# The RWKV-7 recurrence on 64x64 blocks, eight heads a group, its inverse applied to the right-hand sides

## The chip, the cores and the metric

One NeuronCore of a Trainium2 chip runs the whole program; the other cores are idle. The metric is the device time of one execution in microseconds (us). TensorE is called PE here, VectorE DVE, ScalarE ACT, GpSimd POOL. A matmul of float32 operands shows in the trace as two records on PE (and two weight loads on PEld), so "records" below are twice the matmul calls of the code.

## The reference, cut to what matters

The program is a long network on 256 tokens of width 1024: two attention layers with feed-forward blocks, then one RWKV-7 layer, a mixture of 32 experts, one more attention layer and a second mixture. The change touches the RWKV-7 recurrence alone, which every one of the 16 heads (64 channels each) runs on its own:

```python
def wkv7_scan(r, w, k, v, a, b):
    # S_t = S_{t-1} diag(w_t) + (S_{t-1} a_t) b_t^T + v_t k_t^T ;  y_t = S_t r_t.
    def step(state, inp):
        r_t, w_t, k_t, v_t, a_t, b_t = inp
        sa = jnp.einsum('bhij,bhj->bhi', state, a_t)
        state = (state * w_t[:, :, None, :] + sa[..., None] * b_t[:, :, None, :]
                 + v_t[..., None] * k_t[:, :, None, :])
        return state, jnp.einsum('bhij,bhj->bhi', state, r_t)
    ...
y = wkv7_scan(rh, jnp.exp(heads(w_log)), kh, vh, -kk, kk * ah)
ym = y.mean(-1, keepdims=True)
yv = jnp.square(y - ym).mean(-1, keepdims=True)
y = ((y - ym) * lax.rsqrt(yv + GN_EPS)).reshape(B, S, D) * gn_g + gn_b
bonus = (jnp.sum(rh * kh * r_k, -1, keepdims=True) * vh).reshape(B, S, D)
return ((y + bonus) * g) @ w_o, v_first
```

## The kernel before

The 256 tokens are two halves of 128; a half holds two chunks of 64 tokens. Within a chunk the recurrence is solved in closed form: score matrices between the tokens of the chunk (products of decayed r, a, k, b), a unit triangular matrix that has to be inverted, and products of the inverse with the values. Between chunks a state Z of 64x64 a head is carried.

The kernel before holds the matrices of both chunks of a half as one 128x128 block-diagonal matrix for each head; the blocks off the diagonal are zero through the masks. Four heads make a group g (their matrices fill one tile `rk_t[g % 2][n]` of 128x512), and two groups, g and g+1, make a "duo", whose steps alternate, so that one group's copies run beside the other group's products. Four duos follow one another: heads 0-7 and 8-15 of the first half of the tokens, then the same of the second half.

PE runs `rk_steps` (L1237), each step for both groups of the duo, on four PSUM banks a group (`rk_bank`):

- `s_ab`, `s_k` (L1125, L1136): scores, operands of 64 rows (the 64 channels of a head), outputs of 128 rows and 128 or 256 columns; even and odd heads lie in rows 0-63 and 64-127.
- `s_ny` (L1143): masked scores times values. The helper `tall` (L1114) takes 128 rows and makes 64 output rows; first all of chunk 0 (c = 0), then all of chunk 1.
- `s_d2` to `s_tt`: the inverse by products of powers, each `four` (L1107): four matmuls of 128x128x128. Order: d2 and its transpose, d4 and transpose, d8, `at` and `b`, t16 and transpose, f and transpose, f2, gt, tt: 56 matmuls a group.
- `s_uw` (L1192): the inverse `tt` times the rows of `ny` and times `rKK`.
- `s_u(c)`, `s_z(c)` for c = 0, 1 and `s_yb`: the walk over the two chunks, 64x64x64 matmuls, each waiting for DVE's update of u or of Z.

DVE masks the scores (`masked`, L2352, two 128x256 operations each), copies some products from PSUM (`v_copy`, L2384), adds the identity (`plus_one`, L2388), and updates u, y and Z (L2420 to L2442). ACT copies the other products (`rk_copy`, L1622). Every hand-over is a semaphore that counts the steps in the lists `RK_PE`, `RK_DVE`, `RK_ACT` (L102 to L106): PE's step waits (`need`) for DVE's or ACT's copy of the step it reads.

Ahead of each half PE transposes the operands (`rk_transposes`, L1083), and ACT (L1648) and DVE (L2450) copy them to AR and BK; the second half's transposes wait for the `yb` updates of the first. Behind the last duo comes the group norm: POOL (`group_norms`, L2583) does the quarters 0 to 2 as they come free, DVE the last one (L2464 to L2474, 128x512 operations), then PE transposes y (`transposes("y_r")`), multiplies it by `wo_r`, and the layer norm and the experts follow.

Weights stream through a ring of six units of 1 MB, loaded by the SP queue as PE sets units free; the recurrence itself sets none free.

Of the kernel before, what the change touches and what calls it, by code (L numbers as in the profile page):

```python
# [12 lines left out]
ALU = mybir.AluOpType  # L13
# [3 lines left out]
P = 128  # L17
# [33 lines left out]
def shape_constants():  # L51
# [4 lines left out]
    def halves(m):  # L56
# [8 lines left out]
    sub = row // SUB == col // SUB  # L65
# [6 lines left out]
        "sub_lower": sub & (row > col),  # L72
        "sub_upper": sub & (row < col),
        "off_lower": chunk & ~sub & (row > col),
        "chunk_upper": chunk & (row < col),
        "chunk_upto": chunk & (row <= col),
# [25 lines left out]
RK_PE = ["ab", "abt", "k", "ny", "d2", "d2t", "d4", "d4t", "d8", "at", "b", "t16t", "t16", "f", "ft", "f2", "gt", "tt",  # L102
         "u0", "w1", "u_0", "z_0", "u_1", "z_1", "yb"]
RK_DVE = ["de", "dtm", "mk", "d2", "dti", "d4t", "d2i", "d8i", "d4ti", "at", "t16t", "f", "f2i", "fti", "tt", "w1",
          "u_0", "z_0", "u_1", "z_1", "yb"]
RK_ACT = ["ny", "d2t", "d4", "b", "t16", "ft", "gt", "u0"]  # L106
# [90 lines left out]
def build(nc, A, out):  # L197
    ctx = ExitStack()
    with ctx:
# [74 lines left out]
        rk_n = [_tiles[18][:, 0:256], _tiles[18][:, 256:512]]  # L274
# [158 lines left out]
        gn_root = sem("gn_root")  # L433
        gn_done = sem("gn_done")
# [60 lines left out]
        def rk_heads(g):  # L495

            return [(2 * par + pp, par, pp, 2 * (g % 4) + pp, 2 * (2 * (g % 4) + pp) + par)
                    for par in range(2) for pp in range(2)]
# [31 lines left out]

        def rk_cols(buf, g, par):

            v = buf[:].rearrange("p t (r q d) -> p t r q d", q=2, d=HD)
            return v[:, g // 4, 2 * (g % 4):2 * (g % 4) + 2, par, :]
# [115 lines left out]
        def _(pe):  # L650
# [432 lines left out]
            def rk_transposes(t):  # L1083

                pe.wait_ge(rk_in, t + 1)
                if t:
                    for g in (2, 3):
                        rk_wait(pe, "dve", g, "yb")
                        rk_wait(pe, "act", g, "u0")
# [24 lines left out]
            def tall(o, c, c0, lhs, i, rhs, signal):  # L1114

                mm(o[HD * c:HD * c + HD, c0:c0 + HD], lhs[:, i * P + HD * c:i * P + HD * c + HD], rhs, signal=signal)
# [6 lines left out]

            def s_ab(g):
                if g >= 2 and g != 4 and g != 5:  # L1125
                    need(g - 2, "yb", "u0")
                for i, par, pp, r, h in rk_heads(g):
                    q = slice(HD * par, HD * par + HD)
                    mm(rk_bank(g, par)[:, pp * P:(pp + 1) * P], AR[q, r, 0, :], BK[q, r, 0, :],
                       signal=rk_pe[g % 2] if i == 3 else None)  # L1130
                for i, par, pp, r, h in rk_heads(g):
                    q = slice(HD * par, HD * par + HD)
                    mm(rk_bank(g, 2 + par)[:, pp * SEQ:(pp + 1) * SEQ], BK[q, r, 0, :],
                       AR[q, r, :, :].rearrange("p x t -> p (x t)"), signal=rk_pe[g % 2] if i == 3 else None)

            def s_k(g):  # L1136
                need(g, dve="de")
                for i, par, pp, r, h in rk_heads(g):
                    q = slice(HD * par, HD * par + HD)
                    mm(rk_bank(g, par)[:, pp * SEQ:(pp + 1) * SEQ], BK[q, r, 1, :],  # L1140
                       AR[q, r, :, :].rearrange("p x t -> p (x t)"), signal=rk_pe[g % 2] if i == 3 else None)

            def s_ny(g):  # L1143
                need(g, dve="mk")
                for c in range(2):
                    for x, tile in enumerate((5, 6)):
                        for i, par, pp, r, h in rk_heads(g):
                            tall(rk_bank(g, 2), c, x * SEQ + i * HD, rk_t[g % 2][tile], i,
                                 rV[:, g // 4, h * HD:(h + 1) * HD], rk_pe[g % 2] if c and x and i == 3 else None)

            def s_d2(g):
                four(g, 0, 1, 0, True)
                four(g, 1, 0, 1, True)

            def s_d4(g):
                need(g, "d2", "d2t")
                four(g, 0, 4, 3, True)
                four(g, 1, 3, 4, True)

            def s_d8(g):  # L1160
                need(g, "d4t", "d4")
                four(g, 3, 6, 5, True)

            def s_at(g):
                need(g, "d2i", "ny")
                four(g, 0, 3, 1, True)
                need(g, "d4ti")
                four(g, 1, 6, 7, True)

            def s_t16(g):  # L1170
                need(g, "at", "b")
                four(g, 2, 4, 0, True)
                four(g, 3, 0, 4, True)

            def s_f(g):
                need(g, "t16t", "t16")
                four(g, 0, 5, 2, True)
                four(g, 1, 2, 5, True)

            def s_f2(g):  # L1180
                need(g, "f", "ft")
                four(g, 2, 3, 1, True)

            def s_gt(g):
                need(g, "fti")
                four(g, 0, 0, 3, True)

            def s_tt(g):
                need(g, act="gt")
                four(g, 1, 7, 4, True)  # L1190

            def s_uw(g):  # L1192
                need(g, "tt", "ny")
                tt = rk_t[g % 2][2]
                for c in range(2):
                    for i in range(4):
                        tall(rk_bank(g, 2), c, i * HD, tt, i, rk_n[g % 2][:, i * HD:(i + 1) * HD],
                             rk_pe[g % 2] if c and i == 3 else None)
                for i, par, pp, r, h in rk_heads(g):
                    mm(rk_bank(g, 3)[HD * par:HD * par + HD, pp * P:(pp + 1) * P],  # L1200
                       rKK[:, g // 4, h * HD:(h + 1) * HD], tt[:, i * P:(i + 1) * P],
                       signal=rk_pe[g % 2] if i == 3 else None)

            def s_u(c):
                def step(g):
                    need(g, "z_0" if c else "w1", "u0")
                    if g >= 4 and c == 0:
                        need(g - 4, "z_1")
                    t = slice(CH * c, CH * c + CH)
                    for par in range(2):  # L1210
                        for x in range(2):
                            for pp in range(2):
                                r, q = 2 * (g % 4) + pp, slice(HD * par, HD * par + HD)
                                lhs = AR[q, r, 1, t] if x else rk_t[g % 2][6][q, SEQ + pp * P + CH * c:SEQ + pp * P + CH * c + CH]
                                mm(rk_bank(g, par)[t, x * P + pp * HD:x * P + (pp + 1) * HD], lhs, Z[q, r, :],
                                   signal=rk_pe[g % 2] if par and x and pp else None)
                return step

            def s_z(c):
                def step(g):  # L1220
                    need(g, f"u_{c}")
                    t = slice(CH * c, CH * c + CH)
                    for i, par, pp, r, h in rk_heads(g):
                        o = rk_bank(g, 2)[HD * par:HD * par + HD, pp * HD:(pp + 1) * HD]
                        hc = slice(h * HD, (h + 1) * HD)
                        mm(o, rA[t, g // 4, hc], rk_t[g % 2][5][t, i * HD:(i + 1) * HD], True, False)
                        mm(o, rK[t, g // 4, hc], rV[t, g // 4, hc], False, True,
                           signal=rk_pe[g % 2] if i == 3 else None)
                return step

            def s_yb(g):
                for c in range(2):
                    for i in range(4):
                        tall(rk_bank(g, 3), c, i * HD, rk_t[g % 2][8], i, rk_t[g % 2][5][:, i * HD:(i + 1) * HD],
                             rk_pe[g % 2] if c and i == 3 else None)

            rk_steps = [s_ab, s_k, s_ny, s_d2, s_d4, s_d8, s_at, s_t16, s_f, s_f2, s_gt, s_tt, s_uw,  # L1237
# [65 lines left out]
            for g in (6, 7):  # L1303
                rk_wait(pe, "dve", g, "yb")
# [1440 lines left out]
```

## Time and profile before

| | us |
|---|---|
| three runs | 2927.4, 2938.86, 2939.47 |
| median of the three | 2938.86 |
| the profiled execution, its own time | 2947.6 |
| its span in the trace | 2945.7 |
| first score matmul of the recurrence | at 1374.06 |
| last update of y (L2442) ends | at 1589.24 |
| PE busy, share of the span | 85% |

The profiled execution is 8.7 us above the median. In the lists of rows "out<-in" are tiles by the program's names with the buffer numbers left out (B3 is B), `128*64 128x64` on PE is rows times columns of the weights and then partitions times elements of the moving operand; busy is the union of the records' times, the mean is that of one record's length, and a record's length contains some 0.2 us of pipeline, so the rate is read from starts, not from lengths. The time behind "idle before" in brackets names what the engine waited for.

### The profile page before, as it was taken

How to read it: one execution, taken by the hardware profiler on the slowest of the kernel's cores; microseconds unless marked ns; L12 is line 12 of the kernel's file. 1: busy time of each engine (PE TensorE's matmuls, PEld its weight loads, DVE VectorE, ACT ScalarE, POOL GpSimd, SP SyncE). 2: the span in 40 equal slices, each digit the busy share in tenths (PEclk: the TensorE clock that was granted, in tenths of full speed). 3: DMA queues.
4: the chain of work that ended last, by engine and by line, in shares of the span. 5: the costliest groups of instructions: out<-in, count | busy, mean ns of one | idle time of the engine just before them, and what ended most of it. 6: DMA issues, size and time to landing. Idle time of an engine off the chain costs nothing. (4 is left out here: it accounts for less than half of the span.)

```text
span 2945.7 us, 38153 instructions
## 1 busy us (share of the span) xinstructions
PE 2516.4 (85%) x14696; PEld 1765.7 (60%) x14696; DVE 1508.1 (51%) x2095; ACT 721.9 (25%) x1031; POOL 892.5 (30%) x540
## 2 busy tenths in 40 slices
PE   7998769987997799798888689889868868888985
PEld 7986659967996699545886333333347654343432
DVE  7875669768955597427564412222156463212123
ACT  4324433333334333112111110101023321011110
POOL 6888878888800285000233000000001000000000
PEclk9999889988998899897999799999988789999998
DMA  8666347655652365332001499999954127999995
GB/s 296 230 230 218 109 152 256 249 188 210 235 196 77 117 241 215 136 119 90 1 2 44 153 420 420 422 422 421 421 198 143 58 74 321 419 418 422 421 422 249
DMA packets 109853, 694.82 MB, mean 236 GB/s; under 512 B 14424, under 2 KB 15768, under 8 KB 34856
## 3 DMA queue, kind: packets, MB, share of 16 engines
q1 hardware_dynamic: 88704, 618.23, 53.5%
q0 software_dynamic: 21024, 74.99, 7.3%
q8 instruction: 79, 1.29, 0.2%
q14 instruction: 32, 0.25, 0.0%
q10 hardware_dynamic: 14, 0.06, 0.0%
HBM read 692.12 MB, written 1.11 MB: 235 GB/s over the span
## 5 line engine op out<-in xcount | busy, mean ns | idle before, releaser
L666 PE MATMUL bank<-ring,B 128*64 128x512 f32 (+1 forms) x3264 | 781.1, 598 | 113.1 <-DMA ring<-in_moe_wgate 67.8
L1839 DVE TENSOR_TENSOR ring_r<-ring,B_r 128x2048 fp32r<-128x2048 f32 x184 | 539.5, 2951 | 213.2 <-ACT B_r L1400 213.0
L666 PEld LDWEIGHTS bank<-ring,B 128*64 128x64 f32 (+1 forms) x3264 | 269.0, 140 | 582.5 <-issue 569.6
L666 PE MATMUL bank<-B_r 128*128 128x512 f32 (+1 forms) x1928 | 512.0, 352 | 17.5 <-DVE B L2082 9.7
L1400 ACT ACTIVATE B_r<-ring 128x2048 fp32r<-128x2048 f32 x184 | 347.0, 1909 | 322.6 <-PE bank L666 320.1
L666 PE MATMUL bank<-xt_r,B_r 128*128 128x256 f32 x1408 | 401.1, 285 | 23.8 <-issue 8.9
L666 PEld LDWEIGHTS bank<-B_r 128*128 128x128 f32 x1928 | 333.4, 193 | 110.8 <-issue 56.9
L666 PE MATMUL bank<-xt_r,ring_r 128*128 128x256 f32 x1408 | 399.0, 283 | 0.0
L666 PEld LDWEIGHTS bank<-xt_r,B_r 128*128 128x128 f32 x1408 | 269.0, 191 | 26.8 <-issue 24.7
L666 PEld LDWEIGHTS bank<-xt_r,ring_r 128*128 128x128 f32 x1408 | 270.5, 192 | 0.0
L664 PE MATMUL bank<-const,B 128*128 128x128 f32 x688 | 127.9, 351 | 138.2 <-issue 25.0
L666 PE MATMUL bank<-B 128*128 128x128 f32 (+7 forms) x1536 | 188.6, 315 | 40.8 <-DVE B L2355 11.3
L2567 POOL TENSOR_TENSOR wkx<-wkx,small_s 128x1024 f32<-128x1024 f32 x84 | 201.2, 2405 | 66.9 <-DMA wkx<-in_ada_w 55.5
L666 PE MATMUL bank<-B_r,xt_r 128*128 128x512 f32 x416 | 174.9, 421 | 43.0 <-DVE lo_r L1850 23.0
L664 PEld LDWEIGHTS bank<-const,B 128*128 128x128 f32 x688 | 111.2, 188 | 155.6 <-issue 89.9
L666 PEld LDWEIGHTS bank<-B 128*128 128x128 f32 (+4 forms) x1536 | 162.3, 198 | 63.2 <-issue 15.3
L2093 DVE TENSOR_TENSOR B<-bank,B 128x512 f32<-128x512 f32 x128 | 79.7, 683 | 234.5 <-PE bank L666 234.4
L666 PE MATMUL bank<-lo_r,B_r 128*128 128x256 f32 x704 | 199.2, 283 | 0.0
L2120 DVE TENSOR_TENSOR B_r<-bank,B_r 128x512 fp32r<-128x512 f32 x64 | 41.2, 686 | 273.0 <-ACT B_r L1511 273.0
L666 PE MATMUL bank<-ring_r,xt_r 128*128 128x512 f32 x416 | 171.9, 413 | 0.0
L2660 POOL DMA_DIRECT2D rows<-mod_rows x14 | 7.7, 553 | 496.9 <-DVE small_s L1752 462.2
L2111 DVE SCALAR_TENSOR_TENSOR B<-B,bank 128x512 f32<-128x512 f32 x32 | 36.5, 1140 | 226.0 <-issue 185.2
(328 smaller groups left out, 3263.0 us busy)
## 6 DMA issues: line engine op xcount, KB each, us to landing
ring<-in_moe_wgate SPq DMA_DIRECT2D x128, 1024.0 KB, 8.5
ring<-in_moe_wup SPq DMA_DIRECT2D x128, 1024.0 KB, 8.7
ring<-in_moe_wdown SPq DMA_DIRECT2D x128, 1024.0 KB, 9.9
ring<-in_ffn_w_gate SPq DMA_DIRECT2D x44, 1024.0 KB, 4.8
ring<-in_ffn_w_up SPq DMA_DIRECT2D x44, 1024.0 KB, 5.0
ring<-in_ffn_w_down SPq DMA_DIRECT2D x44, 1024.0 KB, 4.9
wkx<-in_ada_w POOLq DMA_DIRECT2D x72, 512.0 KB, 6.0
B<-in_ada_w POOLq DMA_DIRECT2D x24, 512.0 KB, 8.2
```

Of the source, the lines that this page charges most:

```text
L664: ins = pe.transpose(out, lhsT, rhs)
L666: ins = pe.matmul(out, lhsT, rhs, start=start, stop=stop, skip_group_check=True)
L1400: act.activation(hi, ring[:, slot, :], ACT.Copy).then_inc(sp_hi, 1)
L1839: dve.tensor_tensor(ring_r[:, slot, :], ring[:, slot, :], f32(hi), ALU.subtract).then_inc(sp_lo, 1)
L2093: dve.tensor_tensor(y, bank[4 + 2 * t + e][:, :], y, ALU.add).then_inc(mo_acc, 1)
L2111: dve.scalar_tensor_tensor(out=strided(m_h, 4), in0=natural(m_sg, 4), scalar=m_slot[(n // 2) % 2][:, j:j + 1], in1=natural(bank[1][:, :], ...
L2120: dve.tensor_tensor(ye_lo[:, c], bank[2 + d][:, :], f32(ye_hi[:, c]), ALU.subtract)\
L2567: pool.tensor_tensor(w, w, cs[:, 2 * t:2 * t + 2].unsqueeze(2).to_broadcast([P, 2, BANK]), ALU.mult).then_inc(mod_chain, 1)
L2660: pool.dma_start(bc[n % NROW], row_source(name).partition_broadcast(P)).then_inc(row_landed[n % NROW], 16)
```

## The change

- The constant masks shrink from 128x128 to 128x64 (two 64x64 blocks, one for each chunk), and a matrix of 128x128 with two zero blocks becomes a tile of 128x64: rows 0-63 are chunk 0, rows 64-127 chunk 1. A tile of 128x512 so holds eight heads, and a group is eight heads: four groups in all, in two rounds ("half") in place of four duos.
- `four` and `tall` go. `chunks` makes every product: for each of eight heads, a 64x64x64 matmul in rows 0-63 to output rows 0-63, then one in rows 64-127 to output rows 64-127 of the same bank. The scores too are made in 64x64 (or 64x64x128) pieces, alternating over both halves of rows and columns.
- The inverse is not formed. Its last factors are applied to the right-hand sides: `s_f` computes f, its transpose and two products with the right-hand sides (`y`), `s_z1` squares f (transposed) and applies the next factor, `s_uw` the last one. The steps t16, gt, f2 and tt leave; at, d8 and b become single products.
- `s_d2` moves ahead of `s_ny`.
- DVE's and ACT's copies are as wide as before (512 columns) and serve eight heads; some are additions now (`v_plus`, `v_z1`).
- Group norm: POOL does quarters 0 and 1 (the first half), DVE the whole second half in 128x1024 operations, with POOL's gate and bonus for it kept in `lo`.

The diff, cut to its core:

```diff
-            def four(g, x, lhs, rhs, sig):
-                for i in range(4):
-                    c = slice(i * P, (i + 1) * P)
-                    mm(rk_bank(g, x)[:, c], rk_t[g % 2][lhs][:, c], rk_t[g % 2][rhs][:, c],
-                       signal=rk_pe[g % 2] if i == 3 else None)
+            def chunks(o, lhs, rhs, signal, c0=0):
+                for i in range(8):
+                    for c in range(2):
+                        t, x = slice(CH * c, CH * c + CH), slice(i * CH, (i + 1) * CH)
+                        mm(o[t, x], lhs[t, x], rhs[t, c0 + i * CH:c0 + (i + 1) * CH],
+                           signal=signal if i == 7 and c else None)
+            def product(g, x, lhs, rhs):
+                tiles = rk_t[g % 2]
+                chunks(rk_bank(g, x), tiles[lhs], tiles[rhs], rk_pe[g % 2])
+            def scores(g, x, side):
+                v = rk_bank(g, x)[:, :].rearrange("p (r x s) -> p r x s", x=2, s=CH)
+                o = rk_bank(g, x + 1)[:, :].rearrange("p (r x s) -> p r x s", x=2, s=CH)
+                for i, r in rk_pairs(g):
+                    for c in range(2):
+                        t = slice(CH * c, CH * c + CH)
+                        for par in range(2):
+                            q = slice(HD * par, HD * par + HD)
+                            mm((v, o)[par][t, i, :, :], BK[q, r, side, t], both(AR[q, r, :, :], c),
+                               signal=rk_pe[g % 2] if i == 3 and c and par else None)
 ...
+            def s_d2(g):
+                need(g, dve="dtm")
+                product(g, 2, 1, 0)
+                product(g, 3, 0, 1)
 ...
+            def s_at(g):
+                need(g, "dti", "ny")
+                product(g, 0, 3, 1)
             def s_d8(g):
                 need(g, "d4t", "d4")
-                four(g, 3, 6, 5, True)
+                product(g, 1, 6, 5)
+            def s_b(g):
+                need(g, "d8i")
+                product(g, 2, 6, 7)
+            def s_t16t(g):
+                need(g, "b")
+                product(g, 3, 4, 0)
             def s_f(g):
-                need(g, "t16t", "t16")
-                four(g, 0, 5, 2, True)
-                four(g, 1, 2, 5, True)
-            def s_f2(g):
-                need(g, "f", "ft")
-                four(g, 2, 3, 1, True)
-            def s_gt(g):
-                need(g, "fti")
-                four(g, 0, 0, 3, True)
-            def s_tt(g):
-                need(g, act="gt")
-                four(g, 1, 7, 4, True)
+                need(g, act="t16t")
+                product(g, 0, 5, 2)
+                product(g, 1, 2, 5)
+                h, cols = rk_cols(g)
+                chunks(rk_bank(g, 2), rk_t[g % 2][5], rk_n[g % 2], None)
+                chunks(rk_bank(g, 3), rk_t[g % 2][5], rKK[:, h, cols], rk_pe[g % 2])
+            def s_z1(g):
+                need(g, dve="ft")
+                product(g, 0, 1, 3)
+                need(g, act="y")
+                chunks(rk_bank(g, 2), rk_t[g % 2][3], rk_t[g % 2][6], None)
+                chunks(rk_bank(g, 3), rk_t[g % 2][3], rk_t[g % 2][7], rk_pe[g % 2])
             def s_uw(g):
 ...
+                need(g, "z1")
+                product(g, 0, 2, 0)
+                w, tt = rk_t[g % 2][4], rk_t[g % 2][2]
+                for x in range(4):
+                    for c in range(2):
+                        for par in range(2):
+                            i, t = 2 * x + par, slice(CH * c, CH * c + CH)
+                            k = slice(i * CH, (i + 1) * CH)
+                            mm(rk_bank(g, 1 + c)[HD * par:HD * par + HD, x * CH:(x + 1) * CH], w[t, k], tt[t, k],
+                               signal=rk_pe[g % 2] if x == 3 and c and par else None)
 ...
-            rk_steps = [s_ab, s_k, s_ny, s_d2, s_d4, s_d8, s_at, s_t16, s_f, s_f2, s_gt, s_tt, s_uw,
+            rk_steps = [s_ab, s_k, s_d2, s_ny, s_d4, s_at, s_d8, s_b, s_t16t, s_f, s_z1, s_uw,
                         s_u(0), s_z(0), s_u(1), s_z(1), s_yb]
 ...
-            for duo in range(4):
-                if duo % 2 == 0:
-                    rk_transposes(duo // 2)
+            for half in range(TB):
+                rk_transposes(half)
                 for step in rk_steps:
-                    for g in (2 * duo, 2 * duo + 1):
+                    for g in (2 * half, 2 * half + 1):
                         step(g)
 ...
-            h, c, n = quarter(3)
-            y, hs = rR[:, h, c], slice(n, n + 8)
+            y, sq16, hs = heads(rR, 1), B[9][:, 0, :].rearrange("p (h d) -> p h d", d=HD), slice(H, 2 * H)
```

In `s_u` and `s_z` the two halves of rows (or of output rows) alternate matmul by matmul, where before one half's matmuls came first.

## Rows read from the trace of the kernel before

**Rows 1.** The page of the profile: busy time; DMA share in each of 40 slices.

```profile
PE 2516.4 (85%) x14696; PEld 1765.7 (60%) x14696; DVE 1508.1 (51%) x2095; ACT 721.9 (25%) x1031; POOL 892.5 (30%) x540
...
DMA  8666347655652365332001499999954127999995
```

**Rows 2.** Busy time of each engine in stretches; "x" counts instruction records, PEclk is granted clock.

```profile
core 0: us, PE busy (x) PEld busy (x) DVE busy (x) ACT busy (x) POOL busy (x), PEclk, DMA share, GB/s
1374.00:1589.20 215.20, 188.84 (x2208) 179.98 (x2208) 132.08 (x316) 40.84 (x85) 55.01 (x75) 0.97 0.02 5
1374.00:1386.40 12.40, 9.51 (x112) 8.84 (x112) 8.09 (x24) 0.72 (x3) 2.49 (x2) 0.86 0.06 24
1434.00:1441.00 7.00, 7.00 (x76) 6.88 (x75) 1.15 (x4) 1.44 (x6) 6.42 (x8) 0.60 0.01 2
...
1479.00:1485.06 6.06, 3.85 (x36) 3.53 (x34) 3.09 (x7) 2.06 (x4) 4.50 (x9) 1.00 0.01 4
```

**Rows 3.** PE in order of time (start, length, shapes, records, idle before): 128x128x128 products.

```profile
1402.20 1.06 PE L666 MATMUL bank<-xt,wkx 128*128 128x128 f32 x8
1403.10 1.06 PE L666 MATMUL bank<-wkx,xt 128*128 128x128 f32 x8
```

**Rows 4.** The same view: 64-column products, first in one half, then across two.

```profile
1492.64 1.72 PE L666 MATMUL bank<-B 128*64 128x64 f32 x29 [2.83 <-DVE B L2355]
1494.15 0.27 PE L666 MATMUL bank<-B,wkx 128*64 128x64 f32 x1
...
1494.25 0.22 PE L666 MATMUL bank<-B,wkx 128*64 128x64 f32 x1
1494.26 0.22 PE L666 MATMUL bank<-B 128*64 128x64 f32 x1
1494.31 0.22 PE L666 MATMUL bank<-B,wkx 128*64 128x64 f32 x1
1494.32 0.22 PE L666 MATMUL bank<-B 128*64 128x64 f32 x1
```

**Rows 5.** The same view: expert products in two column halves, then full width.

```profile
1761.46 2.79 PE L666 MATMUL bank<-ring,B 128*64 128x512 f32 x12 [0.91 <-DMA ring<-in_moe_wgate]
...
1603.82 2.74 PE L666 MATMUL bank<-ring,xt 128*128 128x512 f32 x6
```

**Rows 6.** Groups of instructions by shape, 1374 to 1600 us: DVE, ACT and one of PE.

```profile
L2384 DVE COPY B<-bank 128x512 f32<-128x512 f32 x24 | 16.5, 688 | 37.7 <-PE bank L666 37.7
...
L666 PE MATMUL bank<-B 64*128 64x256 f32 x128 | 16.2, 384 | 0.0
L1624 ACT ACTIVATE B<-bank 128x512 f32<-128x512 f32 x24 | 14.3, 597 | 53.6 <-PE bank L666 53.6
...
L2355 DVE TENSOR_TENSOR B<-bank,const 128x256 f32<-128x256 f32 x40 | 14.2, 413 | 2.3 <-PE bank L666 2.3
```

**Rows 7.** PE in order of time: the starts at which it had stood idle, and for whom.

```profile
1381.64 0.58 PE L666 MATMUL bank<-B 128*64 128x64 f32 x3 [2.83 <-DVE B L2355]
...
1411.01 0.71 PE L666 MATMUL bank<-B 128*128 128x128 f32 x4 [1.38 <-DVE B L2388]
...
1419.12 0.96 PE L666 MATMUL bank<-B 64*64 64x64 f32 x16 [0.38 <-DVE B L2422]
...
1485.06 0.39 PE L666 MATMUL bank<-B 64*128 64x128 f32 x2 [1.43 <-DVE B L2450]
```

**Rows 8.** DVE in order of time, at the end of the recurrence; last, a 1024-wide group before it.

```profile
1589.33 0.69 DVE L2464 TENSOR_REDUCE small_s<-B 128x8 f32<-128x512 f32 x1
...
1594.35 0.69 DVE L2474 TENSOR_TENSOR B<-B,mix_t 128x512 f32<-128x512 f32 x1
...
L2338 DVE TENSOR_TENSOR B<-B 128x1024 f32<-128x1024 f32 x2 | 2.4, 1216 | 0.0
```

**Rows 9.** The chain that ended last, in order of time, behind the recurrence.

```profile
1595.30 3.65 PE bank L664 x16
...
1599.78 29.54 PE bank L666 x64
```

More of the change, by code:

```diff
@@ L64, in shape_constants @@
     chunk = row // CH == col // CH
-    sub = row // SUB == col // SUB
+    at, to = row % CH, np.arange(CH)[None, :]
+    sub = at // SUB == to // SUB
     aug = p % 64
@@ L1122, in need, with both @@
                     rk_wait(pe, "act", g, act)
-            def s_ab(g):
[L1125 to L1134, printed above, removed]
+            def both(v, c):
+                return v[:, :, CH * c:CH * c + CH]
@@ L1136, in s_k @@
+            def s_ab(g):
+                for i, r in rk_pairs(g):
+                    for c in range(2):
+                        t = slice(CH * c, CH * c + CH)
+                        for par in range(2):
+                            q = slice(HD * par, HD * par + HD)
+                            mm(rk_bank(g, par)[t, i * CH:(i + 1) * CH], AR[q, r, 0, t], BK[q, r, 0, t],
+                               signal=rk_pe[g % 2] if i == 3 and c and par else None)
+                scores(g, 2, 0)
             def s_k(g):
@@ L1137, in s_k @@
                 need(g, dve="de")
[L1138 to L1141, printed above, removed]
+                scores(g, 0, 1)
+            def s_d2(g):
+                need(g, dve="dtm")
+                product(g, 2, 1, 0)
+                product(g, 3, 0, 1)
@@ L1143, in s_ny @@
             def s_ny(g):
                 need(g, dve="mk")
[L1145 to L1153, printed above, removed]
@@ L1204, in s_u @@
             def s_u(c):
                 def step(g):
-                    need(g, "z_0" if c else "w1", "u0")
-                    if g >= 4 and c == 0:
-                        need(g - 4, "z_1")
+                    need(g, "z_0" if c else "z1", "w1")
                     t = slice(CH * c, CH * c + CH)
[L1210 to L1216, printed above, removed]
+                    w = rk_t[g % 2][6][:, :].rearrange("p (r s) -> p r s", r=4)
@@ new lines, in step @@
+                    for side in range(2):
+                        for x, r in rk_pairs(g):
+                            for par in range(2):
+                                q = slice(HD * par, HD * par + HD)
+                                lhs = AR[q, r, 1, t] if side else w[q, x, t]
+                                mm(rk_bank(g, par)[t, side * SEQ + x * HD:side * SEQ + (x + 1) * HD], lhs, Z[q, r, :],
+                                   signal=rk_pe[g % 2] if par and side and x == 3 else None)
@@ L1644, in _ @@
-            for duo in range(4):
-                if duo % 2 == 0:
-                    for b in range(4):
-                        act.wait_ge(wt_pe, 8 * (duo // 2) + b + 1)
-                        act.activation(AR[:, 2 * b:2 * b + 2, :, :].rearrange("p r x t -> p (r x t)"), bank[b][:, :],
-                                       ACT.Copy).then_inc(wt_act, 1)
-                for step in (rk_ny, rk_step("d2t", 4, 1), rk_step("d4", 5, 0), rk_step("b", 4, 1),
-                             rk_step("t16", 7, 3), rk_step("ft", 3, 1), rk_step("gt", 4, 0), rk_u0):
-                    for g in (2 * duo, 2 * duo + 1):
+                h, cols = rk_cols(g)
@@ new lines, in rk_ny, with rk_y, rk_w1 @@
+                rk_copy(g, "ny", rk_n[g % 2], 0)
+                rk_copy(g, "ny", rR[:, h, cols], 1).then_inc(rk_act[g % 2], 1)
+            def rk_y(g):
+                rk_copy(g, "y", rk_t[g % 2][6], 2)
+                rk_copy(g, "y", rk_t[g % 2][7], 3).then_inc(rk_act[g % 2], 1)
+            def rk_w1(g):
+                rk_wait(act, "pe", g, "w1")
+                w = rk_t[g % 2][6][:, :].rearrange("p (r s) -> p r s", r=4)
+                for c in range(2):
+                    v = bank[4 * (g % 2) + 1 + c][:, 0:SEQ].rearrange("p (r s) -> p r s", r=4)
+                    ins = act.activation(w[:, :, CH * c:CH * c + CH], v, ACT.Copy)
+                ins.then_inc(rk_act[g % 2], 1)
@@ new lines, in _ @@
+            for half in range(TB):
+                for b in range(4):
+                    act.wait_ge(wt_pe, 8 * half + b + 1)
+                    act.activation(AR[:, 2 * b:2 * b + 2, :, :].rearrange("p r x t -> p (r x t)"), bank[b][:, :],
+                                   ACT.Copy).then_inc(wt_act, 1)
+                for step in (rk_step("d2", 3, 2), rk_ny, rk_step("d4", 5, 2), rk_step("t16t", 5, 3), rk_y,
+                             rk_step("u0", 5, 0), rk_w1):
+                    for g in (2 * half, 2 * half + 1):
@@ new lines, in v_yb @@
+                h, cols = rk_cols(g)
+                sig(dve.tensor_tensor(rR[:, h, cols], rkb(g, 2)[:, :], rR[:, h, cols], ALU.add), g)
+            for half in range(TB):
+                dve.wait_ge(rk_in, TB)
+                for b in range(4):
+                    dve.wait_ge(wt_pe, 8 * half + 4 + b + 1)
+                    dve.tensor_copy(BK[:, 2 * b:2 * b + 2, :, :].rearrange("p r x t -> p (r x t)"),
+                                    bank[4 + b][:, :]).then_inc(wt_dve, 1)
+                for step in (v_de, v_dtm, v_mk, v_copy("d2t", 4, 3), v_dti, v_copy("d4t", 6, 3),
+                             v_plus("at", 0, 0, "dti", 1), v_one("d8", 7, 1), v_plus("b", 4, 2, "d8i", 7), v_f,
+                             v_copy("ft", 3, 1), v_one("f2t", 2, 0), v_z1, v_u(0), v_z(0), v_u(1), v_z(1), v_yb):
+                    for g in (2 * half, 2 * half + 1):
```

242 lines of the change are left out of this document (109 added, 133 removed).

## The prediction, made before the changed kernel ran

> **What bounds the kernel now.** I read the page first: PE is busy 85% of the span and DMA is the wall only in the expert stages, while around slice 19 to 21 the DMA share is 0 [rows 1]. So in the recurrence nothing but PE and its partners can be late. The stretches say more [rows 2]: from PE's first score matmul to the last update of y pass 215.2 us, in which PE is busy 188.8, DVE 132, ACT 41, and DMA moves 5 GB/s because the ring is full. PE's order of time shows why it is not more [rows 7]: in each duo it waits 2.8 us for the masks (L2355), 1.4 us for an added identity (L2388), 0.4 for u (L2422), the copies after the transposes 1.4 us, and one stretch between the halves takes 6.1 us [rows 2]. The 2.8 us waits also cost clock: behind one, 7 us ran at 0.60 of the full clock [rows 2]. Behind the recurrence the chain runs on through DVE's norm, the transposes and `wo_r` without a gap [rows 8, 9]; the experts' loads wait for units that `wo_r` frees, so a microsecond saved in the recurrence arrives at the end in full. I take that at one to one: the ring is full in both kernels.
>
> **The price of a record.** Everything hangs on this. A 128x128x128 product takes 0.90 us for 8 records, 112 ns each [rows 3]: two passes of the 128 columns. A record with 64 columns takes 0.06 us, 58 before rounding (1494.25 to 1494.31 of one stream) [rows 4]. So half the columns cost half, but half the rows or half the output rows buy nothing by themselves: a 64x64x64 product has 1/8 of the work of a 128x128x128 one and half its price. Eight heads in two chunks need 16 of them (32 records), where eight heads needed 8 full ones (16 records): 32 x 58 = 1.86 us against 16 x 112 = 1.79 us. Without overlap the blocks win nothing.
>
> They do overlap. Where the `tall` products pass from output rows 0-63 to 64-127, two streams run side by side: starts at .25, .26, .31, .32, that is two records in 58 ns [rows 4]. The expert products, which alternate over the two column halves, show it without end: 12 records of 512 columns in 2.79 us, against 6 in 2.74 us at full width [rows 5]. Halves of the rows overlap too: 128 score records of 256 columns and 64 rows were busy 16.2 us, 127 ns each, where two passes of 256 columns alone would take 225 [rows 6]. No row shows a pair that differs in both and writes one bank, as `chunks` makes it, nor more than a few 64-column pairs in line. Bounds for a record: 29 ns (two perfect streams) and 58 ns (one stream). I take 31, by the pair in rows 4, with a little for each first record; 29 to 36 belongs to the forecast.
>
> **Part by part.** *PE.* Before, a group of four heads has 136 matmuls, 56 of them full; eight groups, 2176 records (the trace has 2208 with some neighbours [rows 2]). After, a group of eight heads has ab 32, k 16, d2 32, ny 32, d4 32, at, d8, b and t16t 16 each, f 64, z1 48, uw 32, u and z 64, yb 16: 432 matmuls, 864 records; four groups, 3456 records. At 31 ns that is 107 us of PE, in place of 188.8.
>
> *DVE and ACT.* The copies are as wide as before (690 ns on DVE, 600 on ACT, 413 for 256 columns [rows 6]) and serve twice the heads. A group costs DVE 12 masks at 0.34 us apart, 11 wide operations at 0.60 apart, u and z 2 x 2.0, yb 0.7: about 16 us, 63 for the four. It is no bound in sum. ACT has 10 operations a group, about 6 us.
>
> *The waits.* I walked the new order step by step with these durations, two groups in turn; a step of 32 records is 1.0 us, and the way through a copy and back is 0.26 (pipeline) + 0.69 + 0.05, also 1.0 us, so single-product steps (at, d8, b, t16t) just hide it. The mask wait of 2.8 us goes: `s_d2` needs only dtm and now lies ahead of `ny`, and ab, k and d2 cover DVE's masks but for 0.3 us. `s_z1` is covered by the long `s_f`. The added first wait is z1's for ACT's y: f of the other group (4 us) is queued ahead of it, cost nothing; if it were not hidden it would be 1.2 us twice a half. What is late next is u and z: DVE's four 64x256 operations take 1.4 us against PE's 1.0, so each pass over u and z stands some 0.8 us, together 3.2 us a half. So a half is 1728 x 31 = 53.6, + 3.2 = 56.8 us, + 0.9 for DVE's last yb.
>
> *Between and around.* The 6.1 us between the halves stay [rows 2]; two of the four duo starts vanish with their mask waits. At the start PE is on the low clock (0.86 over the first 12.4 us [rows 2]); I allow 1.5 us. Sum: 56.8 + 6.1 + 57.7 + 1.5 = 122.1 us against 215.2: 93.1 saved.
>
> *Group norm.* DVE's last norm now has 1024 columns: seven operations of 0.70 become 1.22 [rows 8], + 3.6 us, all on the path. POOL's part is shorter and ends in the first half's shadow; its three gate steps at the start (some 15 us) lie beside PE's work and may slow a mask a little, 0 to 1 us. Net 89.5 us. Smaller constants, and the additions in place of copies: nothing.
>
> The profiled execution took 2947.6 us, its like after would be 2858; the runs' median is 8.7 lower, so against it 2938.9 - 89.5 = **2849.4**, I say 2850. At 29 ns a record the walk gives 2844 (stalls grow as PE shrinks), at 36 it gives 2864.
>
> **The rivals.** (a) *The supply of instructions or the turn-around is slower than two full streams*, say 45 ns a record. For it: pairs in line were never seen longer than four, and the rate of records doubles against the 2208 in 215 us. Halves of 78.5 us, net 46 saved: 2893.
> (b) *Two row halves on one bank take turns.* In every place of the old kernel where row halves alternate, they write different banks; `chunks` alone (1216 of a half's 1728 records) writes one. Those at 58 ns, the rest at 31: 86.4 + 1 us a half, 183 in all, net 29 saved: 2910. The Trainium skill, "TensorEngine Tiling (Array Packing)", Restrictions and Gotchas, says this: different row tiles cannot access the same PSUM bank at the same time. By that rule 2910 holds; the trace has no case for or against it, since its overlaps on one bank share their rows.
> (c) *No overlap at all*, 58 ns: halves of 100 us, 209 in all, net 3 saved: 2936. Against it rows 4, 5 and 6.
> The Trainium skill, "TensorE: Matmul & The Clock Gate", section on 56 against 53.3 ns, names a decoding mode in which every matmul costs 62 ns; by that page the sum would be an estimated 214 us for PE and 2949 in all; the two records in 58 ns of rows 4 speak against it.
> (d) *The blocks use less of the array and the clock stays low*, at 1.2 GHz: a pair in 107 ns, 54 each, 196 us, net 16: 2923. Against it: 215 us of mixed shapes had a mean clock of 0.97, and the low stretches follow idle time [rows 2].
> (e) *Every change of half costs a restart: slower.* The first record of a new stream is 0.05 us longer than those behind it (0.27 at 1494.15, 0.22 then [rows 4]). If that were lost time and no overlap came of it, each matmul in `chunks` and its kin would pay it, as the half changes with each; the mean record is then 58 + 25 = 83 ns: 286 us of PE, 82 us more: 3021. It decides from a mean of 58.5 ns on. Against it: the alternating expert products lose nothing [rows 5].
>
> **How the numbers follow.** Forecast 0.66 (2844 to 2864), (a) 0.14, (b) 0.08, (c) 0.04, (d) 0.03, (e) 0.05. The range reaches from 2838 (29 ns, less the 6 us by which a run may lie low) to 2898 (case a and as much above) and leaves out b to e, 0.20. Half a per cent, 15 us, is about what a measurement of this kernel can tell from no change. Faster by more: forecast, a, b and half of d, 0.90. Same: c and the rest of d, 0.05. Slower: e, 0.05.
>
> **What would show it.** In the profile of the changed kernel: PE's records in the recurrence about 3456 at a mean spacing near 31 ns, pairs of starts a few ns apart all through `chunks`; idle spots of PE before u and z, none of 2.8 us; granted clock near 1 past the first microseconds; a norm tail of some 9.5 us in place of 5.9. `chunks` at 58 ns with scores near 30 would be (b); spacing in bursts with no waits between would be (a); a DVE that is never idle would mean that I sized the copies wrong.

## The result, and the profile after

| | before | changed |
|---|---|---|
| median of the runs, us | 2935.48 (4 runs, 2927.4 to 2939.47) | 2851.39 (4 runs, 2836.06 to 2853.56) |
| ratio, with its 95% interval | | 0.9701 (0.9664 to 0.9738) |
| second comparison, on one chip | 2933.11 (11 runs) | 2836.47 (5 runs), ratio 0.9667 (0.9641 to 0.9692) |
| first score matmul to last update of y, us | 215.2 | 113.6 (second profile 114.4) |
| PE idle between y's last matmul and its transposes, us (start to start) | 6.8 | 10.9 |

The changed kernel is 84 us faster by the first comparison, 97 by the second; 2850 was forecast. The page of the changed kernel, where [rows 1] stood before:

```profile
PE 2421.3 (85%) x15976; PEld 1682.0 (59%) x15976; DVE 1432.9 (51%) x1927; ACT 704.3 (25%) x991; POOL 879.8 (31%) x520
...
DMA  7765436765764156533102799999933129999995
```

The windows of the recurrence, to be read beside [rows 2] (the same columns): the whole, its first 5.4 us, the long middle part of the first half, and the stretch between the halves.

```profile
core 0: us, PE busy (x) PEld busy (x) DVE busy (x) ACT busy (x) POOL busy (x), PEclk, DMA share, GB/s
1374.60:1488.20 113.60, 104.84 (x3488) 101.96 (x3488) 70.20 (x148) 23.58 (x45) 43.52 (x55) 1.00 0.03 10
1374.60:1380.00 5.40, 5.18 (x209) 4.92 (x211) 4.65 (x14) 0.00 (x0) 5.09 (x5) 1.00 0.10 39
1380.00:1414.50 34.50, 34.38 (x1206) 34.24 (x1202) 19.02 (x33) 8.62 (x16) 7.80 (x6) 1.00 0.02 4
1427.40:1433.70 6.30, 3.89 (x40) 3.57 (x36) 3.17 (x5) 2.06 (x4) 5.44 (x11) 1.00 0.00 0
```

1280 more records than before, and PE is busy 84 us less: 104.8 against 188.8. What PE was not busy in fell too, from 26.4 to 8.8 us. The clock was at 1.00 from the first score matmul on. The middle part shows the price: 34.5 us with 1206 records, 28.6 ns each, with hardly a pause. In order of time, two steps made by `chunks` (two products each), the step `s_uw`, and the score matmuls with 128 columns (group by shape):

```profile
1383.26 2.03 PE L672 MATMUL bank<-B 64*64 64x64 f32 x64
1385.13 2.03 PE L672 MATMUL bank<-B,wkx 64*64 64x64 f32 x64
...
1411.70 1.61 PE L672 MATMUL bank<-B 64*64 64x64 f32 x64
1413.15 1.03 PE L672 MATMUL bank<-xt 64*64 64x64 f32 x29
```

```profile
L672 PE MATMUL bank<-B 64*64 64x128 f32 x256 | 8.1, 270 | 0.6 <-issue 0.6
```

From 1383.26 to 1385.13 pass 1.87 us for 64 records: 29.2 ns each, the price of `chunks`. In `s_uw` (from 1411.70 to 1413.15) the first 32 records are a product of `chunks`, some 0.93 us at that price; the other 32, w1, use all four quarters of the array in turn and have the remaining 0.52 us, about 16 ns each. They draw the mean of the middle part down. 256 score records were busy 8.1 us, 32 ns each, though each has twice the columns; the scores use all four quarters too.

PE's order of time, the longer waits, first half and the stretch behind it (beside [rows 7]):

```profile
1379.48 2.08 PE L672 MATMUL bank<-B 64*64 64x64 f32 x64 [0.22 <-DVE xt L2375]
...
1415.59 1.15 PE L672 MATMUL bank<-Z,B 64*64 64x64 f32 x32 [0.87 <-ACT B L1661]
...
1418.24 1.15 PE L672 MATMUL bank<-B 64*64 64x64 f32 x32 [0.57 <-DVE B L2451]
...
1423.20 1.15 PE L672 MATMUL bank<-B 64*64 64x64 f32 x32 [0.36 <-DVE B L2451]
...
1428.57 3.68 PE L670 MATMUL bank<-const,B 128*128 128x128 f32 x32 [0.99 <-DVE B L2469]
```

The 2.8 us for the masks are 0.22; what is late is now ACT's copy of w1 (0.87), then DVE's u (0.57 and 0.36). The wait for yb ahead of the transposes is 1.0 us, where it was 0.8. In the second profile the same waits stand in the same places; only ACT's is shorter in the first half, 0.56. DVE's norm at the end, beside [rows 8]; in between lie the like rows at 1489.52, 1490.78 and 1492.04 and 0.8 us of small operations:

```profile
1488.27 1.22 DVE L2486 TENSOR_REDUCE small_s<-B 128x16 f32<-128x1024 f32 x1
...
1494.03 1.23 DVE L2494 TENSOR_TENSOR B<-B,small_s 128x1024 f32<-128x1024 f32 x1
1495.29 1.23 DVE L2496 TENSOR_TENSOR B<-B 128x1024 f32<-128x1024 f32 x1
1496.55 1.23 DVE L2497 TENSOR_TENSOR B<-B,lo 128x1024 f32<-128x1024 f32 x1
```

### The profile page after: what moved, and what is told of

Same layout as the page of the kernel before. It is cut to its first block, busy times and chain, and to the rows that moved or that the text cites. A ratio compares the mean times of both kernels' runs of the same rounds, so it can differ in the third digit from the quotient of the medians.

```text
span 2834.2 us, 40407 instructions
## 1 busy us (share of the span) xinstructions
PE 2421.3 (85%) x15976; PEld 1682.0 (59%) x15976; DVE 1432.9 (51%) x1927; ACT 704.3 (25%) x991; POOL 879.8 (31%) x520
## 4 chain that ended last, share of the span: by engine, by line
PE 48%; DMA 26%; DVE 9%; POOL 8%; issue 6%; ACT 2%; SPq 1%; POOLq 0%; DVEq 0%; ACTq 0%
PE bank L672 46%; DMA ring<-in_moe_wup 11%; DMA ring<-in_moe_wgate 11%; POOL wkx L2592 2%; DMA wkx<-in_ada_w 2%; PE bank L670 2%; POOL wkx L2596 2%; POOL wkx L2598 1%; DVE ring_r L1857 1%; POOL B L2592 1%; SPq L582 1%; POOL mix_t L2601 1%; POOL B L2604 0%; DMA B<-in_ada_w 0%; DMA const<-in_const 0%
## 5 line engine op out<-in xcount | busy, mean ns | idle before, releaser
L1857 DVE TENSOR_TENSOR ring_r<-ring,B_r 128x2048 fp32r<-128x2048 f32 x184 | 526.7, 2882 | 221.1 <-ACT B_r L1416 220.8
L672 PE MATMUL bank<-B 64*64 64x64 f32 (+6 forms) x2272 | 126.8, 253 | 20.2 <-ACT B L1480 5.4
L672 PE MATMUL bank<-ring_r,B_r 128*128 128x512 f32 x352 | 138.9, 395 | 0.0
```

Source lines behind the costliest of these rows:

```text
L672: ins = pe.matmul(out, lhsT, rhs, start=start, stop=stop, skip_group_check=True)
L1857: dve.tensor_tensor(ring_r[:, slot, :], ring[:, slot, :], f32(hi), ALU.subtract).then_inc(sp_lo, 1)
```

## The experiments

### The price of a stream by itself

The kernel `bench` leaves out everything of the reference: it holds only streams of 64 float32 matmuls (128 records), each behind a short wait. Its loop (`row half`, `output half`, bank, columns, for matmul i):

```python
s["one"]       = [(0, 0, 1, 64)] * n
s["diagonal"]  = [(i % 2, i % 2, 2, 64) for i in range(n)]
s["same_rows"] = [(0, i % 2, 3, 64) for i in range(n)]
s["same_out"]  = [(i % 2, 0, 4 + i % 2, 64) for i in range(n)]
s["four"]      = [(i % 2, (i // 2) % 2, 6 + i % 2, 64) for i in range(n)]
s["runs2"]     = [((i // 2) % 2, (i // 2) % 2, 2, 64) for i in range(n)]   # runs4, runs8 alike
s["four_32"]   = [(i % 2, (i // 2) % 2, 6 + i % 2, 32) for i in range(n)]
```

> Only streams of float32 matmuls of 64x64x64, 64 of them (128 records) each, nothing of the reference is computed. Spacing of records in ns that the theory expects (two streams in different row or output halves run side by side; a stream alone takes 58; the engine looks about four records ahead): one tile 58; the two diagonal tiles in turn on one bank 29; same rows, output halves in turn, one bank 29; rows in turn, same output half, two banks 29; all four tiles in turn 15; diagonal in runs of 2 matmuls 29; runs of 4, 29 to 36; runs of 8, about 45; four tiles with 32 columns 15, if the weight load of 64 columns is as long as the matmul, 8 if not. Rival (one bank is shared badly by two row halves): the first diagonal stream at 58. Rival (the supply of instructions ends somewhere near 29): all four tiles no faster than 25.

PE in order of time, one row a stream in the order one, diagonal, same_rows, same_out, four, runs2, runs4, runs8, four_32:

```profile
22.58 7.67 PE L62 MATMUL bank<-X 64*64 64x64 f32 x128 [0.40 <-DVE t L71]
30.57 3.95 PE L62 MATMUL bank<-X 64*64 64x64 f32 x128 [0.32 <-DVE t L71]
34.85 3.95 PE L62 MATMUL bank<-X 64*64 64x64 f32 x128 [0.33 <-DVE t L71]
39.13 3.95 PE L62 MATMUL bank<-X 64*64 64x64 f32 x128 [0.33 <-DVE t L71]
43.41 2.21 PE L62 MATMUL bank<-X 64*64 64x64 f32 x128 [0.33 <-DVE t L71]
45.96 4.16 PE L62 MATMUL bank<-X 64*64 64x64 f32 x128 [0.35 <-DVE t L71]
50.44 4.99 PE L62 MATMUL bank<-X 64*64 64x64 f32 x128 [0.32 <-DVE t L71]
55.74 6.42 PE L62 MATMUL bank<-X 64*64 64x64 f32 x128 [0.32 <-DVE t L71]
62.48 2.07 PE L62 MATMUL bank<-X 64*64 64x32 f32 x128 [0.32 <-DVE t L71]
```

This is one execution; its granted clock was 1.00 in the window of each of these streams. A row's length, less the 0.22 us of its last record, over 127 steps: 58.7 ns for one tile; 29.4 for the diagonal on one bank, for two output halves and for two row halves; 15.7 for all four tiles; runs of 2, 4 and 8 matmuls 31.0, 37.6 and 48.8; four tiles with half the columns 14.6. So a tile (a quarter of the array, 64 rows by 64 output rows) takes 58.7 ns a record alone and the same beside one other; with all four at work it takes 62.8 (4 x 15.7), so the tiles are all but independent. The diagonal on one bank is as fast as any pair, so the rival of the shared bank falls. The last stream shows that instructions can come at one record in 14.6 ns. With 32 columns a record is nearly as long as with 64: what is left is the weight load of 64 columns, or the rate of supply, which this run does not tell apart. A run of 8 matmuls (16 records) takes 16 x 48.8 = 781 ns where alone it would take 939: the next tile begins some 160 ns, nearly three records, ahead of the end. The expected spacings were met within 4 ns; the runs of 2, 4 and 8 came out the dearest against them (29, 29 to 36 and about 45 were expected).

### The same work, one half of the array after the other

```diff
-                for i in range(8):
-                    for c in range(2):
+                for c in range(2):
+                    for i in range(8):
                         t, x = slice(CH * c, CH * c + CH), slice(i * CH, (i + 1) * CH)
```

> The changed kernel with the two loops in chunks swapped: all eight heads of chunk 0 first, then all eight of chunk 1. The same matmuls, copies and waits; only the order within a product differs. Theory (the gain is the overlap of the two halves of the array, and a new stream starts when about four records of the old one are left): a chunks record costs (32 - 4) x 58 / 32 = 51 ns instead of 29; 2432 such records, + 53 us of PE, of which 3 to 5 us fill stalls that exist already: about + 48, 2900 us. Rival (the gain comes from fewer waits, fewer rounds and the cheaper algebra, the order within a product is indifferent): within 5 us of the changed kernel, 2851. Second rival (no overlap unless matmuls alternate one by one): 58 ns, + 66, 2917.

Measured: 2892.37 us, ratio 0.982 (0.9762 to 0.9878), in its own comparison with the kernel before (2935.07). Against the changed kernel's ratios, 0.9701 and 0.9667, that is 35 and 45 us more. Windows of its recurrence, the whole and the long middle part of the first half:

```profile
1371.79:1529.50 157.71, 149.46 (x3488) 146.91 (x3488) 69.06 (x148) 24.11 (x45) 42.75 (x55) 0.99 0.02 8
1376.68:1432.08 55.40, 55.40 (x1215) 55.40 (x1216) 19.29 (x34) 8.73 (x16) 7.53 (x7) 1.00 0.01 3
```

The recurrence took 157.7 us, 44.1 more than the changed kernel's 113.6, from two swapped loops. In the middle part 1215 records take 55.4 us, 45.6 ns each, w1 among them. Steps made by `chunks` alone, 64 records each, follow one another every 3.02 us (at 1382.94, 1385.95 and 1388.97): 47.1 ns a record. 51 was expected; 48.8 is what `bench` gives for runs of eight matmuls. The 17.9 ns above 29.2, for 2432 such records, make 43.5 us, nearly the whole difference. The look-ahead is seen as well: from 1382.71 to 1382.88 the last three records of one tile start in turn with the first three of the next. Idle time is 8.3 us, where it was 8.8. The rival that the order is indifferent falls; so does the one that needs strict alternation (58 ns).

The second kernel orders the scores, u, z and w1 so too (each loop over the halves `c` and `par` pulled outside the loop over the heads, as above):

> As the last one, and the scores, u, z and w1 are also ordered so that each quarter or half of the array gets all its matmuls before the next one does. Theory: on top of the 51 ns of chunks, the scores go from 21 to about 56 ns a record (runs of 8 records, 4 of them overlapped), u and w1 to 36, z to 51: together 171 us of PE against 100, less 5 us of stalls filled: + 66, about 2917. If it comes out at 2936 or above, the 64x64 form without overlap wins nothing or loses, as the prediction's case c says. If it stays below 2880, the recurrence got shorter for another reason than overlap.

Measured: 2899.32 us, ratio 0.9868 (0.9815 to 0.992).

```profile
1372.50:1545.40 172.90, 167.98 (x3488) 166.77 (x3488) 69.54 (x148) 24.00 (x45) 42.67 (x55) 1.00 0.02 6
```

PE busy 168.0 us, where 171 was worked out; the recurrence took 172.9, + 59.3. The 2917 expected in all was too much by 18 us: the recurrence grew by 59 and not 66, and the 2917 was built on the changed kernel's first median, which lay 15 us above its second. Against the kernel before the recurrence is still 42.3 us shorter: 20.9 of PE and 21.4 of idle time; less the 4.1 us of the longer norm that makes 38, and the medians differ by 36 (2935.07 to 2899.32). That PE's share is a gain at all is put down to what the look-ahead hides at each change of tile (48.8 against 58.7 ns, or 1.56 us a product of eight heads against the 1.79 of [rows 3]); the other share is the waits. A 64x64 form with no overlap whatever could not be made, since the engine looks ahead by itself; by an estimate from `bench` it would cost 3456 x 58.7 = 203 us of PE, more than the old form's 188.8. This also speaks against the new algebra as the cause: counted in products of eight heads, the inverse and its application were 16 before and are 17 now (w1 and u0 taken in), so applying the factors instead of forming the inverse saves PE none of them. What it does for the waits was not tried by itself.

### The overlap alone, in the kernel before

The kernel before with its 64-row and 64-column matmuls in turn; `rk_heads` lists the heads with `par` inside, and `tall` is called with `c` inside:

```diff
-                for c in range(2):
-                    for i in range(4):
+                for i in range(4):
+                    for c in range(2):
                         tall(rk_bank(g, 3), c, i * HD, rk_t[g % 2][8], i, rk_t[g % 2][5][:, i * HD:(i + 1) * HD],
```

(the same in `s_ny` and `s_uw`; in `s_u` and `s_z` the loop over `par` goes innermost)

> The kernel before, block-diagonal 128x128 matrices and all, with one thing of the change alone: its 64-row or 64-column matmuls (scores, ny, uw, u, z, yb) alternate between the two halves, one by one. Theory: ny, uw and yb fall from some 50 to 30 ns a record, u and z are soon held by DVE's updates: 3 to 4 us a duo, together - 12 us (- 8 to - 18), 2923 us. Rival (the new order alone is worth a large part of the 84 us): below 2900. Rival (DVE's waits take it all back): within 3 us of 2935.

Measured: 2930.73 us, ratio 0.9976 (0.9948 to 1.0005), 12 runs.

```profile
1366.60:1572.90 206.30, 175.26 (x2208) 163.92 (x2208) 133.15 (x317) 40.86 (x85) 56.10 (x75) 0.97 0.02 5
```

The recurrence took 206.3 us, 8.9 less. PE is busy 13.6 us less, and 4.7 of that comes back as idle time. Of that 2.2 us stand before the added identity (12.0 in all against 9.8, the longest 2.3 against 1.4), since DVE's work ahead of it takes as long as before, and only 0.3 before u (2.7 against 2.4). The rival of a large part (below 2900) falls. The other (within 3 us of 2935) can't be refuted by the timing, whose interval reaches from 15 us less to 1 more; it is the trace that shows the 8.9 us. The order pays only where matmuls leave a part of the array free: 112 of the 272 records of a group were full 128x128 ones with nothing to run beside.

### The step that was moved

```diff
-RK_PE = ["ab", "abt", "k", "d2", "d2t", "ny", "d4",
+RK_PE = ["ab", "abt", "k", "ny", "d2", "d2t", "d4",
-            rk_steps = [s_ab, s_k, s_d2, s_ny, s_d4,
+            rk_steps = [s_ab, s_k, s_ny, s_d2, s_d4,
```

(and ACT copies ny ahead of d2)

> The changed kernel with s_ny ahead of s_d2, as in the kernel before. Theory (the move hides DVE's masks): PE ends k at 4.4 us, the masks for ny are ready 7.7 us after the first score matmul, so PE stands 3.3 us in each half where it stood 0.5; + 2.8 twice, and if the idle time brings the low clock back as in the kernel before, some 2.5 us more in each half: + 6 to + 10, 2857 to 2861. Rival (the masks are hidden anyway, for the copies behind would wait the same): + 0 to + 1.

Measured: 2859.74 us, ratio 0.9726 (0.9673 to 0.9779). Two waits of PE, and windows of the whole recurrence and of the 6 us behind the first wait:

```profile
1379.94 3.53 PE L672 MATMUL bank<-B 64*64 64x64 f32 x64 [2.87 <-DVE B L2375]
...
1443.12 2.48 PE L672 MATMUL bank<-B 64*64 64x64 f32 x64 [2.28 <-DVE B L2375]
```

```profile
1372.40:1493.50 121.10, 107.74 (x3488) 104.68 (x3488) 68.77 (x148) 23.58 (x45) 42.59 (x55) 0.97 0.03 9
1379.90:1386.00 6.10, 6.06 (x158) 6.06 (x160) 1.31 (x4) 1.70 (x4) 5.10 (x5) 0.73 0.01 3
```

The wait for the masks is back, 2.9 and 2.3 us, and behind the first one the clock is 0.73. The recurrence took 121.1 us, + 7.5: 4.6 more idle time and 2.9 more busy time for the same records. The latter is the clock: it is 0.73 in the 6.1 us shown, 0.75 in the 6.9 behind the second wait (from 1443.1), and 1.00 in the long stretches behind each. The rival (+ 0 to + 1) falls. In the timing the step is worth 0 to 1% and the interval does not part it from nothing; the trace does.

### Two waits shortened

```diff
-                    for par in range(2):
-                        b = rkb(g, par)[t, :]...
-                        u = by_parity(rk_t[g % 2][5][t, :], par)
-                        dve.tensor_tensor(u, b[:, 0, :, :], u, ALU.add)
-                        y = by_parity(rR[t, h, cols], par)
-                        ins = dve.tensor_tensor(y, b[:, 1, :, :], y, ALU.add)
-                    sig(ins, g)
+                    b = [rkb(g, par)[t, :]... for par in range(2)]
+                    for par in range(2):
+                        u = by_parity(rk_t[g % 2][5][t, :], par)
+                        ins = dve.tensor_tensor(u, b[par][:, 0, :, :], u, ALU.add)
+                    sig(ins, g)
+                    for par in range(2):
+                        y = by_parity(rR[t, h, cols], par)
+                        dve.tensor_tensor(y, b[par][:, 1, :, :], y, ALU.add)
 ...
+                for g in (2 * half, 2 * half + 1):
+                    rk_step("u0", 5, 0)(g)
+                    rk_w1(g)
```

(`v_yb` now waits for z_1 instead of u_1, since y is added later.)

> The changed kernel with two waits shortened. DVE tells PE of u as soon as both u additions are done and adds y afterwards, and ACT copies u0 and w1 of one group before it turns to the other. In the changed kernel's trace PE stands before u_0 for 1.09 us, before z_0 for 0.79 and before z_1 for 0.57 (start to start, of which 0.06 is a normal step), in each half. Theory (these are waits for the copies, and DVE has room behind them): they fall to about 0.3, 0.2 and 0.1, 1.8 us a half, 3.6 in all: 2848, too little for the timing, but plain in the trace: recurrence from 113.4 to about 110 us. Rival (DVE is the bound in u and z, and what PE gains in front it waits behind): less than 1 us in all.

Measured: 2834.83 us, ratio 0.9661 (0.9633 to 0.9689); the changed kernel on the same chip 2836.47 and 0.9667. PE's waits in the first half, from u and z, and the window of the whole recurrence:

```profile
1424.72 0.33 PE L672 MATMUL bank<-wkx,B 64*64 64x64 f32 x4 [0.18 <-DVE wkx L2451]
...
1426.17 1.15 PE L672 MATMUL bank<-Z,B 64*64 64x64 f32 x32 [0.31 <-DVE Z L2465]
```

```profile
1381.49:1492.00 110.51, 104.22 (x3488) 101.66 (x3488) 69.52 (x148) 23.61 (x45) 43.27 (x55) 1.00 0.03 10
```

The wait for w1 is gone, those for u are 0.2 us; a new one for Z (0.3) stands ahead of u_1, because DVE now adds y in front of its update of Z. The recurrence took 110.5 us, 3.1 less than in the changed kernel's first profile and 3.9 less than in its second. That is the theory's size (3.6, to about 110 us), and what comes back as the rival says is the 0.3 us a half before Z. It is the fastest version here, but the timing can't part it from the changed kernel.

### The changed kernel once more

> The changed kernel once more, for its time and a second profile. The recurrence and its norm are 97.8 us shorter in the first profile, the medians differ by 84 to 88 us. Theory (the 10 us are scatter of the DMA-bound stages, 15 us between single runs): the recurrence again 113.4 us long from first score matmul to last update of y, ratio 0.967 to 0.971. Rival (a later stage gives 10 us back): the stages behind the transposes of y are about 10 us longer than in the kernel before.

Measured: 2836.47 us, ratio 0.9667 (0.9641 to 0.9692). What lies behind the start of y's transposes, in the kernel before, the changed one, and the changed one's second profile (here with its recurrence):

```profile
1595.30:2945.70 1350.40, 1113.95 (x5384) 570.57 (x5384) 422.00 (x806) 204.50 (x383) 46.59 (x37) 0.93 0.78 320
```

```profile
1498.09:2834.20 1336.11, 1100.36 (x5384) 562.83 (x5384) 420.04 (x806) 204.29 (x383) 44.77 (x37) 0.94 0.79 323
```

```profile
1370.01:1484.40 114.39, 105.66 (x3488) 102.39 (x3488) 70.18 (x148) 23.58 (x45) 43.49 (x55) 1.00 0.03 10
1494.30:2846.00 1351.70, 1114.45 (x5384) 572.12 (x5384) 422.07 (x806) 204.37 (x383) 46.59 (x37) 0.93 0.78 319
```

From the first score matmul to y's transposes passed 221.2 us before (1374.06 to 1595.30) and 123.5 after (1374.60 to 1498.09): 97.7 saved. In the second profile it was 124.3, the recurrence 114.4 and not again 113.6: 97.0 saved. The stages behind took 1350.4, 1336.1 and 1351.7 us with the same 5384 records and the same bytes; in the middle one PE was busy 14 us less at a clock of 0.94 in place of 0.93. So the rival finds no support: two executions of one kernel differ there by 15 us and lie on both sides of the kernel before, of which there is one profile, and the 84 of the first comparison differs from 97 by no more than that. A few microseconds given back by a later stage would not show in these profiles. The interval of the first comparison, 22 us wide, is of the same size.

## Why the prediction was right

**What bounds the kernel.** Right. The time went out of PE's records and PE's waits in the recurrence, and within what the timing can tell all of it arrived at the end: 97.7 us in the trace, 84 and 97 in the two comparisons.

**The price of a record.** This carried the forecast and it held: one tile 58.7 ns, two side by side 29.4, all through `chunks` (29.2 in the kernel). The step that weighed "two records in 58 ns" from a handful of overlapping rows [rows 4] against the long expert stream [rows 5] was the right one; the 31 taken was 1.8 ns too dear in `chunks`, 4.4 us for 2432 records. The scores were mis-sized: at 31 they were priced like `chunks`, but they use all four tiles, and ran at 23 ns (192 records, whose starts lie between 1374.60 and 1379.0), 3.1 us for the 384 of the four groups. w1, at 16 ns, gives some 2 more.

**No gain without overlap.** Right in sign, but the engine's look-ahead gives a part of the overlap to any order: in `one_stream` the recurrence was still 42 us shorter than in the kernel before, where the working "without overlap the blocks win nothing" would have had 6. Case c (2936) supposed an engine without that look-ahead, and falls.

**The waits.** The masks' wait went, as walked (0.22 us left, 0.3 expected), and `ny_first` shows that it was the move that did it, with 2.9 us of clock besides. The walk had u and z as the next to be late: they are, with 3.2 us a half expected and 0.87, 0.57, 0.36, 0.22 and 0.18 found in the first; what it did not name is that the longest of them is ACT's copy of w1. The allowance of 1.5 us for a low clock at the start rested on a wrong reading: the 0.86 over the first 12.4 us [rows 2] does not come from the start. In the kernel before, the clock was 1.00 from 1374.06 to 1378.80, and 0.65 from 1381.60 to 1386.40, behind the wait for the masks. That wait is gone, and the low stretch with it.

**The sum.** 122.1 us for the recurrence were worked out, 113.6 came, 8.5 less: PE was busy 50.4 and 50.8 us in the two halves against 53.6 (6.0 less), stood idle 1.0 us less than walked, and the 1.5 for the clock fell away; the 6.1 between the halves stayed. The norm was put at + 3.6, it was + 4.1. Net 89.5 against 97.7 in the trace. That the median then lay 1.4 us from the forecast is partly luck: the second comparison's median, 2836.47, lies 1.5 us below the range's low end. The range was drawn from a single level of the stages behind; their 15 us of scatter should have been in it on both sides.

**The rivals.** (a) a slow supply: out, records came at 14.6 ns. The Trainium skill, "TensorE: Matmul & The Clock Gate", section "Wait — 56ns, not 53.3ns?", gives about 62 ns a matmul for the mode without hardware decoding. In that mode none of the faster streams could be: on four tiles a matmul, two records, took 31 ns. The traces disagree with it here. (b) row halves that share a bank: out for tiles that also differ in their output half, 29.4 ns on one bank, as fast as the pair of row halves on two. The Trainium skill, "TensorEngine Tiling (Array Packing)", Gotcha 1, states it without that exception; the measurement decides for this pair. Two row halves writing one bank in the same output half was not tried. (c) see above. (d) the clock: out, 1.00 over the whole recurrence in both profiles. (e) a restart at each change of tile: out, runs of 1 are the fastest of all.

## What to carry to other kernels

Count a float32 matmul of up to 64x64x64 by its tile, not by its work: in `bench` each quarter of the array passed one record in about 59 ns on its own (63 with all four at work), so the cost of a step is the load of the fullest quarter, and the order in which the matmuls are written decides how many quarters run. Splitting a block-diagonal product pays mostly through that alternation (29.2 instead of 47.1 ns a record from two swapped loops, 44 us here). When PE gets twice as fast, look next at the signals of the copies: send them after what PE needs, not after the whole step, and give the masks' wait something to hide behind, for here 4.6 us of such idle time cost another 2.9 in clock.

## What was not expected of the hardware

- All four 64x64 tiles run at once, at 15.7 ns a record; the forecast counted on two. The recurrence's products keep each chunk on its own diagonal tile and so use half of that; whether heads could be laid out to use the other two was not tried.
- With 32 columns in place of 64 a record on four tiles takes 14.6 in place of 15.7 ns: halving the columns gains almost nothing there. Fewer than 32 were not tried.
- A tile's next run begins about three records (160 ns) before the other tile's run ends, so runs of 2 matmuls still reach 31.0 ns, runs of 4 reach 37.6.
